# Loading the up pass's expert tiles in pairs: one transfer of 1 MB for two tiles, in a ring of four slots

## What is computed

```
q  = (xt @ wq).reshape(t, 8, 2, 128)
s  = einsum('thpc,pnc->thpn', q, subkeys)      # 2 x 128 scores a head
...                                            # top 16 of each half, top 16 of their 256 sums
eidx = ia * 128 + ib ; gate = softmax(cv)
hc  = gelu(einsum('chkd,cd->chk', u[eidx], x))
out = einsum('chk,chkd->cd', hc * gate, v[eidx])
```

## Time and profile before

| | |
|---|---|
| median of 3 runs | 3456.17 us |
| the profiled execution | 3455.42 us |
| its span, first to last instruction | 3453.6 us |
| mean granted TensorE clock | 0.939 |
| busy: PE / DVE / POOL / ACT | 89% / 75% / 47% / 40% |
| up pass of layer 0, its first tile to its last | about 430 to 1125 us |
| up pass of layer 1 | about 2169 to 2864 us |

### The profile page before, as it was taken

How to read it: one execution, slowest core, us unless ns; L and a number is a source line. 1 busy time by engine, 2 the same in 40 slices (tenths; PEclk the granted TensorE clock), 3 DMA queues, 4 the chain that set the end, 5 groups by cost and what they waited for, 6 DMA issues and landing times.

```text
span 3453.6 us, 46653 instructions
## 1 busy us (share of the span) xinstructions
PE 3077.7 (89%) x17142; PEld 2786.4 (81%) x17142; DVE 2603.6 (75%) x5039; ACT 1373.3 (40%) x2513; POOL 1620.5 (47%) x1157
## 2 busy tenths in 40 slices
PE   6865959999999899999787789499999998999996
PEld 5765959999999688888684679499999997888885
DVE  3745999976653799999657349899766646999997
ACT  2312214466665233333334222144666653333332
POOL 3441239877776234333230032299777763333340
PEclk9977979999999999999897799799999999999998
DMA  3354239999998999999220022299999989999993
GB/s 96 97 26 56 65 127 362 349 360 374 343 347 307 377 412 404 412 410 406 99 74 18 7 61 63 87 344 361 369 359 367 337 311 381 409 405 411 409 410 129
DMA packets 297411, 927.21 MB, mean 268 GB/s; under 512 B 36640, under 2 KB 86560, under 8 KB 293392
## 3 DMA queue, kind: packets, MB, share of 16 engines
q1 hardware_dynamic: 164016, 418.78, 35.2%
q0 software_dynamic: 111280, 404.77, 31.0%
q10 hardware_dynamic: 21888, 100.67, 7.2%
HBM read 820.48 MB, written 105.53 MB: 268 GB/s over the span
## 4 chain that ended last, share of the span: by engine, by line
PE 61%; DVE 25%; DMA 8%; issue 2%; ACT 2%; POOL 2%; SPq 0%; DVEq 0%; ACTq 0%; POOLq 0%
PE ps L1442 31%; PE ps L1390 14%; PE ps L1340 8%; PE ps L1422 4%; DMA rowsB<-u,pick 3%; DVE rowsB L959 2%; DVE rowsA L959 2%; POOL low L490 1%; DMA hOut<-hlast 1%; DMA sring<-s_dram 1%; DVE cand L1024 1%; DVE cand L1031 1%; DVE si L913 1%; DVE si L902 1%; DMA rowsA<-u,pick 1%
## 5 line engine op out<-in xcount | busy, mean ns | idle before, releaser
L611 ACT ACTIVATE high<-raw 128x1024 fp32r<-128x1024 f32 x512 | 541.9, 1058 | 918.4 <-PE ps L1442 686.6
L1390 PE MATMUL ps<-xh,high 128*128 128x384 f32 x2048 | 706.7, 345 | 60.3 <-POOL low L490 60.1
L490 POOL TENSOR_TENSOR low<-raw,high 128x1024 fp32r<-128x1024 f32 x256 | 613.8, 2398 | 255.6 <-ACT high L611 252.7
L1390 PE MATMUL ps<-xh,low 128*128 128x384 f32 x2048 | 690.6, 337 | 0.0
L1390 PE MATMUL ps<-xl,high 128*128 128x384 f32 x2048 | 689.7, 337 | 0.0
L1442 PE MATMUL ps<-high,hh 128*128 128x512 f32 x1536 | 483.8, 395 | 27.0 <-DVE low L1103 27.0
L1442 PE MATMUL ps<-low,hh 128*128 128x512 f32 x1536 | 482.0, 395 | 0.0
L1442 PE MATMUL ps<-high,hl 128*128 128x512 f32 x1536 | 480.7, 394 | 0.0
L1390 PEld LDWEIGHTS ps<-xh,high 128*128 128x128 f32 x2048 | 389.2, 190 | 68.3 <-POOL low L490 66.5
L1390 PEld LDWEIGHTS ps<-xl,high 128*128 128x128 f32 x2048 | 389.3, 190 | 0.0
L1390 PEld LDWEIGHTS ps<-xh,low 128*128 128x128 f32 x2048 | 388.0, 189 | 0.0
(11 more groups left out here) (234 smaller groups left out, 5190.0 us busy)
## 6 DMA issues: line engine op xcount, KB each, us to landing
raw<-uT SPq DMA_DIRECT2D x256, 512.0 KB, 6.9
raw<-v SPq DMA_DIRECT2D x256, 512.0 KB, 10.3
s_dram<-sring ACTq DMA_DIRECT2D x128, 384.0 KB, 7.1
gate_dram<-gblk ACTq DMA_DIRECT2D x24, 2048.0 KB, 11.1
gt<-gate_dram SPq DMA_DIRECT2D x32, 1536.0 KB, 15.8
sring<-s_dram SPq DMA_DIRECT2D x128, 384.0 KB, 10.6
raw<-wts SPq DMA_DIRECT2D x76, 512.0 KB, 3.6
rowsB<-u,pick POOLq DMA_INDIRECT x192, 8.2
```

What stands on the lines that cost most here:

```text
L490: pool.tensor_tensor(low[:, m % 4], raw[:, m % 4], high[:, (m + 2) % 3].bitcast(F32), ALU.subtract).then_inc(sem("lo_ready"), 1)
L611: act.activation(high[:, (m + 2) % 3], tile_raw(m), ACT.Copy).then_inc(sem("hi_ready"), 1)
L1390: ins = pe.matmul(ps[:, m % 2, 0:DN], w[:, c], x[:, c, 0:DN], start=(c == 0 and k == 0), stop=(c == NC - 1 and k == 2))
```

## The change

The loop over m in `experts` of `block.sync` goes in steps of two. One DMA loads tiles m and m + 1 into slots m % 4 and m % 4 + 1, and waits until both slots are free. Each of the two semaphores `t_loaded0` and `t_loaded1` counts one pair of slots; ScalarE waits for the pair's semaphore in `high_tile`, for either tile of the pair. The number of bytes, the runs of 4 KB a partition and tile, the ring and the memory stay the same.

```diff
-                for m in range(KEYS):
-                    if m < 2:
-                        spq.wait_ge(sem("w_split"), splits_made(w_end - 2 + m))
-                    elif m < 4:
-                        spq.wait_ge(sem("tile_done"), d_end - 3 + m)
+                for m in range(0, KEYS, 2):
+                    if m == 0:
+                        spq.wait_ge(sem("w_split"), splits_made(w_end - 1))
+                    elif m == 2:
+                        spq.wait_ge(sem("tile_done"), d_end)
                     else:
-                        spq.wait_ge(sem("mm_done"), after("mm_done", l, m - 3))
-                    spq.dma_start(raw[:, m % 4], uT[l, m].rearrange("p (c e) -> p c e", c=NC)
-                                  ).then_inc(sem(f"t_loaded{m % 4}"), 16)
+                        spq.wait_ge(sem("mm_done"), after("mm_done", l, m - 2))
+                    spq.dma_start(raw[:, m % 4:m % 4 + 2],
+                                  uT[l, m:m + 2].rearrange("t p (c e) -> p t c e", c=NC)
+                                  ).then_inc(sem(f"t_loaded{m // 2 % 2}"), 16)
...
             def high_tile(l, m):
                 if m < KEYS:
-                    act.wait_ge(sem(f"t_loaded{m % 4}"), 16 * (l * KEYS // 4 + m // 4 + 1))
+                    act.wait_ge(sem(f"t_loaded{m // 2 % 2}"), 16 * (l * KEYS // 4 + m // 4 + 1))
```

## The result

The changed kernel takes 3699.69 us (median of 4 runs, 3692.86 to 3706.27), the kernel before on the same chip 3453.03 us. The ratio is 1.0712, with a 95% interval from 1.0689 to 1.0736: some 246 us slower. The profiled executions differ by 3704.5 - 3453.6 = 251 us of span.

A forecast was written before the change was run, and what follows sets the result against it. In stretch A of the up passes PE, DVE, POOL and DMA were taken as all full. 31 + 26 + 8 + 12 + 3 = 80 us a layer, 160 for two, on 3455.4 gave 3615 us; range 3505 to 3725.

The forecast's parts named there:

- rival 2: Up passes: POOL's lead is used up and the loop over gathered rows binds earlier; 3695 us, beyond to 3753; chance 0.14.
- Room after the change, e + L + 3.7: Up passes: tile m of a pair starts 3.7 us after its load, issued at e (end of tile m - 3), lands.
- L in A: Landing time of a 1 MB pair load in tiles 8 to 45: 8.2 us, bounds 6.4 and 10.15.
- Stretch A: Up pass, tiles 8 to 45: 19 pairs at 10.15 us against 8.5, +31 us a layer, bounds +14 and +50.
- Stretch B: Up pass from tile 46 on: 38 pairs at 11.25 us against 10.6, +26 a layer; late landings +8, gathers +12.
- the 12 us for the gathers: Stretch B: late pairs use up POOL's lead, so gathers go out later; +12 us a layer, bounds 0 and 30.
- rival 3: Up passes: pairs land as fast as needed; 3405 us if faster, 3455 if unchanged; chance 0.03 each.
- late landings: Stretch B: the slowest loads, beside the gates' 2 MB stores, cost half their delay; +8 us a layer, bounds 0 and 30.
- The granted clock should stay near 1.00 in A: PE in stretch A: no clock loss in the sum; 1 us more for each late pair only in the upper bounds.
- Ends: First tiles and tiles 123 to 127 of each up pass: +2 and +3 were weighed, +3 us a layer taken, bounds 0 and 5.
- 1 (the landing hardly grows): Pair loads land in about 7 us in both stretches, as queues empty; 3500 to 3515 us; chance 0.16.
- 4 (fewer engines): The pair's transfer is spread over fewer than 16 DMA engines, landings double, time beyond 3750 us; chance 0.01.

The follow-up runs named there:

- number 12: The changed kernel with the gathers of u rows from tile 45 on issued a little ahead: 3676.6 us, 1.0662 of the kernel before.
- number 5: The changed kernel with a ring of six slots, gates in blocks of 16 and five query buffers: 3441.8 us, 0.9967 of the kernel before.
- number 1: The changed kernel with two 512 KB loads, each with its own semaphore, issued at the pair's time: 3538.3 us, 1.0251 of the kernel before.

## Why the prediction was right, and where it was short

The sign, the mechanism and the range held (3505 to 3725; measured 3700), but the forecast of 3615 us was 85 us low, and 3700 lies outside the likeliest case of 3540 to 3680. It lies beside the 3695 of rival 2, whose mechanism number 12 rules out: that agreement is chance.

- **Room after the change, e + L + 3.7**: as predicted, to 0.1 us (tile 20). That cover decides and not the size of the transfer is shown by number 5, and both halves, the later issue and the merged landing, by number 1.
- **L in A**: 8.2 was taken; 9.1 is what counts (8.8 in layer 1), since only every second pair is late and those are the slow landings. The median of all is 7.7 in A and 7.5 in B, so the 8 to 9 us that the prediction wanted to see there did not come. The lower bound of 6.4 was no floor: the load of the earlier trace rows ran beside others, at a DMA share of 0.91 from its issue to its landing, and the quickest pair took 4.8. The upper bound of 10.15, worked out from the earlier trace rows, is what the load takes at the old pace (10.2 in number 5).
- **Stretch A**: +31 us a layer predicted. Measured +50 and +53, of which the idle time is 35 and 35. (The window of the earlier trace rows, 507 to 660 us, holds tiles 6 to 41 and not 8 to 43, and 679 to 881 us ends at tile 84; the pace read from them is right.)
- **Stretch B**: 26 + 8 + 12 = 46 a layer predicted. Measured +70 and +54, of which idle time before the gates 48.6 and 38.6. The place is ACT's order, as predicted. That the sum is near the idle time is in part luck: the 12 us for the gathers, and the 50 us of rival 3, rest on 25.2 us of PE's time lost before the gates in the earlier trace rows, which is 11.9 for the matmuls alone (the prediction's own 12 of 196 us in the earlier trace rows), and number 12 leaves no room for a large growth of the gathers' cost. The split between late landings and the rest wasn't measured. I had also written that idle time before the gates and not before L1391 would speak for rival 2, and that sign was wrong: it stands there because ACT waits for the load.
- **The step that failed is the clock.** "The granted clock should stay near 1.00 in A", and the sum has no term for it. It fell to 0.90 in A. The same work takes 15.7 + 21.5 us more of PE's time in layer 0 and 18.3 + 15.7 in layer 1, some 71 of the 91 us that the sum of the profiled execution is short. The idle time of both layers in A and B grew by 157 us, where the terms for A and B made 154; the other 17 are at the ends. The prediction named one tile of 5.21 us behind a gap as the only one, put 1 us a late pair into the upper bounds and nothing into the sum, and spread the loss as 1.7 us on each pair; the gaps came as 2 to 6 us on every second one. And it wasn't the only one: in the kernel before, tile 5 takes 7.3 us behind a gap of 27.8 (499.9 to 507.1 us) and tile 112 of layer 0 takes 6.1 (granted clock 0.73 from 1045 to 1052 us). With their price the term could have been written down.
- **Ends**: +3 a layer predicted. Up to tile 8 the passes take 11 and 5 us more, up to 8 us of that at tile 8 itself, the first late pair (a gap of 5.6 and a tile of 6.6 us in layer 0), and behind tile 122 5 and 7 more. Outside the passes it is 5 less.
- **Rivals**: 1 (the landing hardly grows) was right about the median of the landings and wrong about the time. 2 (the gather loop takes over) is excluded by number 12, by the bound set there. 3 (no slower) fell: beside the other traffic the pair took 7.7 us in the middle of A and up to 13.4 in B. The Trainium skill ("DMA: Bandwidth & Descriptors", "Anatomy of one DMA — SWDGE (gpsimd) path") has a fit for transfers issued on GpSimd's path, and 4.4 us for 1 MB is an estimate from it; these loads are issued from SyncE. The quickest pair here landed in 4.8 us, near that estimate, and the others did not. 4 (fewer engines) fell: landings did not double.

## What to carry to other kernels

Merging two loads into one in a ring of the same size takes a tile of cover from the first of them, since the transfer waits for the last slot and signals with its last byte. Count the cover in tiles before and after (here 12.7 against 11.1 us needed, then 8.4 against 12.8), and merge only if the ring grows with it. When a wait breaks through to TensorE, price the gap twice, as idle time and as slow matmuls behind it, and ask whether small gaps will gather into fewer long ones.

## What the runs showed of the hardware that wasn't expected

- With pairs in four slots the loads fell into a pattern in A, at a DMA share of 0.80: one pair late (9.1 us), the next quick (6.2), the quick one being issued while PE and POOL stand still for the late one. With pairs in six slots, at a share of 0.98, both kinds took 10 us. That the missing traffic of PE's and POOL's work makes the quick one quick wasn't tested. A median of landings hides the pattern.
- Behind gaps of 1.8 to 6.4 us a tile took up to 7.3 us instead of 4.4 (granted clock 0.57 over it), though not behind every such gap, and a fill of otherwise useless matmuls kept the clock up. Before tile 32 of layer 1 PE stood still for 1.8 us only; its first four matmuls still came at the higher level, then the clock fell.
- Storing and reading back the gates in half as large blocks (1 MB stores, runs of 512 bytes on the way back), together with five query buffers instead of six, made the kernel 0.35% faster (number 7), though the reads back take 18.3 us instead of 15.8: the down pass hides them, at 538.9 us against 537.7. Where the gain comes from isn't shown; in the one profiled execution of each, 11 us of it lie in B of layer 0, and 5 before the first up pass.
